# A decoder layer on one core: four modulation vectors accumulated on VectorE in place of TensorE

## What is computed

```python
c_act = jax.nn.silu(c)
mod = (c_act @ w_ada[l] + b_ada[l])[:, None, :]
sh1, sc1, g1, sh2, sc2, g2 = jnp.split(mod, N_MOD, axis=-1)
h = x * (1.0 + sc1) + sh1
mix = hybrid_mixer(h, ...)          # h @ w_in, attention, SSD, @ w_out
x = layer_norm(ALPHA * x + (1.0 + g1) * mix, ln1_g[l], ln1_b[l])
h = x * (1.0 + sc2) + sh2
ffn = peer_ffn(h, ...)
x = layer_norm(ALPHA * x + (1.0 + g2) * ffn, ln2_g[l], ln2_b[l])
```

## Time and profile before

| what | value |
| --- | --- |
| median of three runs | 3496.76 us (3495.52 to 3498.98) |
| the profiled execution's own time | 3501.67 us |
| its span, first to last instruction | 3499.6 us |
| mean granted TensorE clock | 0.966 of full speed |
| busy over the span: PE, DVE, ACT, POOL | 91%, 67%, 30%, 26% |
| matmuls of the four later vectors (L1699) | 68.8 us |
| units 33 to 182 in the trace | 199.1 to 850.9 us |

### The profile page before, as it was taken

One profiled execution on the slowest core, in us unless ns is written; L12 is line 12 of the kernel. 1 busy time (PEld: TensorE's weight loads), 2 busy tenths in 40 slices (PEclk: granted clock), 3 DMA queues, 4 the chain that ended last, 5 costly groups with the idle time before them and its releaser, 6 DMA issues.

```text
span 3499.6 us, 45811 instructions
## 1 busy us (share of the span) xinstructions
PE 3189.5 (91%) x16301; PEld 2696.6 (77%) x16301; DVE 2346.8 (67%) x3421; ACT 1060.7 (30%) x1591; POOL 906.4 (26%) x702
## 2 busy tenths in 40 slices
PE   5799999999799876849999999999999999999993
PEld 2576787666448766847789999999999999999982
DVE  1242464744717796676667778778778778778788
ACT  1132455421313233222223333333323333333332
POOL 0010000000005331501103334344344344343340
PEclk9899999999899999979999999999999999999997
DMA  8767213465134243356777888888888888888883
GB/s 311 266 227 250 67 55 127 150 237 178 30 126 129 97 156 122 124 206 206 227 212 257 300 303 291 299 307 286 300 308 283 303 305 287 300 304 288 302 295 149
DMA packets 267984, 784.94 MB, mean 224 GB/s; under 512 B 117616, under 2 KB 125936, under 8 KB 221936
## 3 DMA queue, kind: packets, MB, share of 16 engines
q1 hardware_dynamic: 212720, 459.52, 40.0%
q0 software_dynamic: 50560, 317.87, 24.6%
q10 hardware_dynamic: 4608, 6.29, 0.5%
HBM read 743.76 MB, written 39.85 MB: 224 GB/s over the span
## 4 chain that ended last, share of the span: by engine, by line
PE 72%; issue 14%; DVE 6%; DMA 4%; POOL 3%; ACT 1%; SPq 0%; POOLq 0%; ACTq 0%; DVEq 0%
PE ps L2078 29%; PE ps L2005 24%; PE ps L1734 12%; POOL split L720 3%; DMA arena<-in_w_ada 2%; PE ps L1699 2%; DVE arena L1521 1%; PE ps L1758 1%; PE ps L1793 1%; DMA below_parts<-acts_ahead 1%; PE ps L1672 1%; DVE arena L1518 1%; PE ps L1770 0%; DVE arena L1540 0%; DVE arena L1278 0%
## 5 line engine op out<-in xcount | busy, mean ns | idle before, releaser
L2078 PE MATMUL ps<-split,w_parts 128*128 128x512 f32 x4608 | 1063.7, 391 | 55.1 <-DVE split L1589 36.5
L2005 PE MATMUL ps<-h_parts,split 128*128 128x384 f32 x6144 | 1085.5, 336 | 30.4 <-POOL split L720 30.0
L2005 PEld LDWEIGHTS ps<-h_parts,split 128*128 128x128 f32 x6144 | 1071.9, 189 | 40.9 <-issue 31.8
L2078 PEld LDWEIGHTS ps<-split,w_parts 128*128 128x128 f32 x4608 | 865.8, 188 | 239.9 <-DVE split L1589 37.5
L1040 ACT ACTIVATE split<-below_parts 128x1024 fp32r<-128x1024 f32 x448 | 475.6, 1062 | 1298.9 <-PE ps L2078 741.9
L1589 DVE TENSOR_TENSOR split<-below_parts,split 128x1024 fp32r<-128x1024 f32 x448 | 548.7, 1225 | 398.9 <-ACT split L1040 395.1
L732 POOL COPY arena<-arena 128x1 uint32 x256 | 185.7, 725 | 1069.8 <-DVE arena L1564 543.4
L1134 DVE TENSOR_TENSOR win_parts<-arena,win_parts 128x512 fp32r<-128x512 f32 (+2 forms) x208 | 129.5, 630 | 312.2 <-ACT win_parts L783 303.0
L1564 DVE SCALAR_TENSOR_TENSOR arena<-arena 128x2048 f32<-128x2048 f32 x128 | 300.5, 2348 | 2.7 <-DVE arena L1556 2.2
L720 POOL TENSOR_TENSOR split<-below_parts,split 128x1024 fp32r<-128x1024 f32 x64 | 178.5, 2793 | 441.2 <-ACT split L1004 441.2
L1545 DVE CUSTOM_DVE_ANT_0 arena<-arena 128x2048 f32<-128x2048 f32 x128 | 292.4, 2284 | 0.3 <-DMA arena<-in_u_tab,arena 0.3
(11 more groups left out here) (253 smaller groups left out, 2952.5 us busy)
## 6 DMA issues: line engine op xcount, KB each, us to landing
below_parts<-in_u_units SPq DMA_DIRECT2D x256, 512.0 KB, 4.6
below_parts<-in_v_tab SPq DMA_DIRECT2D x256, 512.0 KB, 6.7
arena<-in_w_ada SPq DMA_DIRECT2D x96, 1024.0 KB, 7.0
arena<-in_w_slices POOLq DMA_DIRECT2D x56, 512.0 KB, 3.9
gates_by_expert<-arena SPq DMA_DIRECT2D x24, 1024.0 KB, 3.9
below_parts<-gates_by_expert SPq DMA_DIRECT2D x32, 768.0 KB, 8.8
arena<-in_w_out POOLq DMA_DIRECT2D x32, 512.0 KB, 5.1
below_parts<-in_w_q SPq DMA_DIRECT2D x16, 512.0 KB, 3.5
```

The source lines that it names most:

```text
L2005: ins = nc.tensor.matmul(ps[:, 6 + b, 0:DT], lhs[:, cols], h2_parts[:, rhs, k, :], start=k == 0 and n == 0, stop=k == KT - 1 and n == 2)
L2078: ins = nc.tensor.matmul(ps[:, 2 * m + b, :], w_parts[:, buf, lhs, i, m * P:(m + 1) * P], rhs[:, b * 512:(b + 1) * 512], start=i == 0 and ...
```

## The change

A part moves from TensorE to VectorE. There it is one instruction over a whole tile: the tile times the 128 values of `c_act` (one for each partition), added to a row of sums in SBUF, `acc` for the first two vectors and `later_acc` for the others. The first part of a vector writes the row and adds nothing. TensorE keeps the sum over the partitions, 16 matmuls of one column as before, now with ones as the right side. ScalarE's four copies go. The bias add moves from VectorE's step of the sum to the one behind it.

```diff
@@ ScalarE, beside(n)
-                if n + 1 in SUMS_AT:
-                    i = SUMS_AT[n + 1]
-                    act.wait_ge(ada_used, 2 * KT + (i + 1) * KT)
-                    nc.scalar.activation((acc if i < 2 else later_acc)[:, 0:512], ps[:, 7, :], ACT.Copy).then_inc(ada_row, 1)
@@ VectorE
+            def later_part(n):
+
+                i, k, tile = n // KT, n % KT, 2 * KT + n
+                if n < 2 * KT:
+                    what, full, count = ada[:, tile % 4, :], ada_full[tile % 4], 16 * (tile // 4 + 1)
+                else:
+                    what, full, count = later_ada[:, tile % 2, :], ada_full[tile % 2], 16 * (KT + (n - 2 * KT) // 2 + 1)
+                to = acc if i < 2 else later_acc
+                dve.wait_ge(full, count)
+                if k == 0:
+                    dve.wait_ge(mod_sum, CHUNKS + i)
+                    ins = nc.vector.tensor_scalar(to, what, c_act[:, k:k + 1], None, ALU.mult)
+                else:
+                    ins = nc.vector.scalar_tensor_tensor(to, what, c_act[:, k:k + 1], to, ALU.mult, ALU.add)
+                ins.then_inc(ada_used, 1)
+                dve.wait_ge(ada_used, tile + 1)
@@ VectorE, beside(n)
-                if n in SUMS_AT:
-                    modulated(SUMS_AT[n])
+                if n in LATER_AT:
+                    later_part(LATER_AT[n])
+                if n - 1 in SUMS_AT:
+                    modulated(SUMS_AT[n - 1])
@@ TensorE
-            def later_part(n):
...
-                for a in range(CHUNKS):
-                    ins = nc.tensor.matmul(ps[32 * a:32 * a + 32, 7, :], c_act[:, k:k + 1].to_broadcast([P, 32]), what[:, a * CW:(a + 1) * CW],
-                                           start=k == 0, stop=k == KT - 1, tile_position=(0, 32 * a))
-                ins.then_inc(ada_used, 1)
-
             def later_sums(i):
 
                 from_acc = acc if i < 2 else later_acc
-                pe.wait_ge(ada_row, 2 * CHUNKS + i + 1)
+                pe.wait_ge(ada_used, 2 * KT + (i + 1) * KT)
+                pe.wait_ge(mod_ready, CHUNKS + i)
+                if i == 2:
+                    pe.wait_ge(row_ready, 4)
                 for k in range(KT):
-                    a, part = k // CK, slice(k % CK * P, (k % CK + 1) * P)
-                    ins = nc.tensor.matmul(ps[:, 7, k:k + 1], from_acc[:, part], ident[:, 32 * a:32 * a + 1], start=True, stop=True)
+                    ins = nc.tensor.matmul(ps[:, 7, k:k + 1], from_acc[:, k * P:(k + 1) * P], ones[:, 0:1], start=True, stop=True)
                 ins.then_inc(mod_sum, 1)
@@ TensorE, beside(n)
-                if n in LATER_AT:
-                    later_part(LATER_AT[n])
                 if n in SUMS_AT:
                     later_sums(SUMS_AT[n])
```

## The result

The changed kernel takes 3502.40 us (median of 17 runs, 3497.91 to 3512.81), the kernel before 3496.59 us beside it (17 runs, 3494.70 to 3500.14). The ratio is 1.002, 95% interval 1.0012 to 1.0027: a small loss, where 3479 was forecast. The profiled execution took 3503.49 us with a span of 3501.4, 1.8 more than the span before. The 4.0 us that this differs from the medians' 5.8 are the profiled executions themselves: that of before lies 5.1 us above its median, that of after 1.1.

What follows compares the result with a forecast made beforehand. TensorE was taken to bound the touched steps, except the SSD stage, where waits pass between engines. Terms -5.6 - 14.4 - 3.6 + 16 - 13.5 + 3.6 = -17.5 us gave 3484.2, as median 3479; forecast's own range 3468 to 3491.

Steps and rivals of the forecast that it cites:

- The cost of a part: Each part costs TensorE 1.2 us before the change; on VectorE 2.35 us, or 1.23 us for a vector's first part.
- the second vector: Steps 58 to 79: TensorE stays the bound and gains 14.4 us to step 73; the sum then moves 3.6 earlier.
- The SSD stage: Steps 133 to 155: VectorE's added parts delay the chain of waits between engines, a loss of 16 us.
- about 20 can take parts: Steps 133 to 155: of VectorE's 42.6 us idle, about 20 can hold parts, so the loss lies between its bounds.
- The first rival: VectorE's idle time takes all parts (-6 in the SSD stage) and loads keep up (-16.8): 3454 us, chance 0.13.
- The third rival: Every part lands on the SSD stage's chain (+36.5) and TensorE's lower clock costs 10: 3510 us, chance 0.12.
- Steps 159 to 182: Fourth vector, steps 159 to 181: 16.8 us can go, late loads take back half of 6.6, a gain of 13.5.
- Each group's end refills the buffers: Steps 159 to 181: the reason given for counting only half of the 6.6 us that late tile loads could take back.
- The first vector: Steps 33 to 55: VectorE becomes the bound; the sum begins at 270.3 instead of 275.95, a gain of 5.6 us.
- Steps 183 and 184: Steps 183 to 185: the last bias add now stands behind `mixed_in`, so unit 185 begins later, a loss of 3.6 us.
- The second rival: Nothing gained: VectorE bounds wherever it has own work, SSD stage +26, loads take their full 6.6; 3502 us, chance 0.20.
- the prediction's own signs: Core wrong if the first sum starts where it did, or the SSD stage grows by under 6 or over 26 us.

## Why the prediction was wrong

**The cost of a part and the second vector: right.** The 60 additions take 2.35 us at the median. TensorE stayed the bound in steps 58 to 73 (busy 47.40 of 47.40 us), and the second vector gave -16.2 for -18.0. The rule of the Trainium skill, Vector Engine (DVE) Microarchitecture Reference, section "Points that are easy to get wrong", by which this form with two such sources is at half throughput, isn't borne out in any of the traces.

**The SSD stage: right in mechanism, 3.9 us too small.** "Those waits turn into parts, and behind the parts the waits for products stay": this is what the waits show, and both runs of the vector alone and of the rest without it confirm the 20 us. VectorE stood still 27.2 of 144.5 us and not 22, and the waits for products were 12.0 us and not 7.5; TensorE's 16.4 us for the masks are the other side of the same chain. But the forecast took the order within a step as given and asked only how much of VectorE's idle time parts could fill ("about 20 can take parts", of 42.6). The run with the parts behind the masks shows that nearly all could: VectorE 115.8 us busy of 123.0. The first rival's "VectorE's idle time takes all the parts" was true of the work, and false of its place. The third rival priced the lower clock on top. The clock fell as it said (0.98 to 0.86), without a price that can be shown inside the stage.

**Steps 159 to 182: the failing step, -4.2 for -13.5.** "At most that takes 1 us per two tiles back, 6.6 us; ... so I take half." The loads took 9.1, the difference to the run that has half the bytes and no broadcasts ahead (-13.3), and not 3.3: this term was mis-sized, and above its own bound. The landing time was read right (6.8 and 6.6 us). The -13.3 looks like the forecast's 13.5 by luck: without waits for loads the forecast was 16.8. The other 3.5 are about what TensorE waits more for `mixed_in` in that run, 9.4 us where it was 5.7. What the forecast missed is what stands in the same queue. SyncE issues two broadcasts of 1 MB between the tiles; before the change a tile had slack enough for them, after it the next tile came 7.27 us late. The order of the queue alone is worth 1.3 to 3.3 us (steps 159 to 181 are between -4.5 and -6.5 in the five traces with it). Each mend alone gave little (-5.8, -7.3) and both together -13.3, since each leaves the other's waits: with the long one gone there are eight short ones, 11.2 us, which I read as the two buffers' turn. "Each group's end refills the buffers" was an assumption that no row bore.

**The first vector: the start right, the net -1.2 for -5.6.** The sum began where it was forecast. The step that failed is the one left out: a wait of 4.84 us for the last part is not only late, it lets TensorE's clock fall, and the sum costs 3.3 us more and unit 57 2.4 more. I had weighed the clock for the stretch of steps 33 to 55, where it stayed at 1.00, and not for the wait ahead of the sum. The Trainium skill, TensorE: Matmul & The Clock Gate, Part 1, says that the clock comes back only with sustained activity; the trace agrees, the sum and the unit behind it are slow, the one after is not. Filler brought back 2.7 of it. Real work in the wait's place brought 7.5 (5.9 with what steps 58 to 80 gave back): 3.8 us less of wait, 2.0 less of the sum, the rest in the units around it. So both are in it, the clock and the time stood still.

**Steps 183 and 184: right, 2.4 us too small.** The cause is shown by the run that undoes it (-0.6). The missing 2.4 us are again the clock behind a wait: the first spread took 2.08 us instead of 1.05, and unit 184 was slower too.

**The second rival had the time and not the reasons.** It said 3502, and 3502.40 was measured. That is luck: of its pieces the SSD stage (+26 for +19.9) and the loads (-10.2 for -4.2) were both off, and the first vector lost its gain to the slow sum and the unit behind it more than to VectorE's lead. By the prediction's own signs its core held: the first sum moved forward (from 275.95 to 268.56, 5.7 us counted from step 33), and the stage grew by between 6 and 26.

**What stays open:** why the third vector alone cost 27 us at the median and 20 in its stage, and what makes a sum behind a short wait fast in one trace and slow in another. Behind waits of 0.7 to 1.5 us the sums took from 3.73 to 6.08 us in the traces of the changed kernels.

## What to carry to other kernels

- Work moved to an engine with room is paid by where it stands in that engine's order. The same 16 instructions of 2.35 us cost 20 us ahead of what another engine waits for, and nothing in the same stage behind it. Ask for each one which instruction behind it has someone waiting.
- A stretch that gets faster wants its transfers sooner: read everything that the same queue issues between them, not only the landing time of one.
- Where a change leaves TensorE waiting some microseconds ahead of short work, count with the lower clock for that work and the unit behind it, or move a unit into the wait.

## What the runs showed that I had not expected

- TensorE ran 32 one-column passes in 6.99 us behind a wait of 4.84 us, 3.66 without one, 5.02 behind a wait of 1.05, and 4.32 behind filler of 4.72 us and a wait of 0.28. The wait just ahead doesn't decide it alone: 3.77 behind one of 1.32, 5.44 behind one of 0.35.
- VectorE can be busy 94% of a stretch of 123 us in a chain over three engines without making it longer (115.8 of 123.0, the stage 1.6 us shorter than before).
- Over the SSD stage with the parts last, a granted clock of 0.89 instead of 0.98 showed no price (stage 123.0 us, 124.6 before; TensorE busy 108.4). Right behind it the third sum took 5.69 us in place of 3.73, and steps 156 to 158 3.9 us more.
- Filler in the SSD stage left the granted clock at 0.86, with TensorE busy 129.2 of 150.3 us (115.2 of 144.5 without filler, also 0.86).
